# Retention values centred at their eviction, and gate tiles one ahead in both gated stages

## The chip, the cores and the metric

The kernel runs on one core of one Trainium2 chip. The metric is the device time of one execution in microseconds (us). The names used are those of the profile: PE is TensorE (matmuls; PEld its weight loads), DVE is VectorE, ACT is ScalarE, POOL is GpSimd, SP is the engine whose queue issues the weight transfers. "Line" or L with a number is a line of the kernel's source.

## What is computed

Two blocks follow one another on 512 tokens of width 1024. The first is an RWKV mixer with dilated attention, a cross attention and a feed-forward part; the change doesn't touch it. The second has two layers, and each of them does this:

```python
n = rmsnorm(x) * (1 + sc1) + sh1
u, q, k, v, g, gate_f, gate_r = split(n @ w_in)
yf = fourier_mix(u)                       # FFT over tokens and over groups of 128 features
yr = retention_branch(q, k, v, g)         # 4 heads of width 256
merged = sigmoid(gate_f) * (yf @ w_fourier) + sigmoid(gate_r) * (yr @ w_ret)
x = x + g1 * (merged @ w_out)
x = x + g2 * conv_ffn(rmsnorm(x) * (1 + sc2) + sh2)
```

In the retention branch a head's output is Y = P V, where P (512 by 512) holds the rotated queries times the rotated keys, weighed by a decay that depends on the distance in tokens. Y is then normalised over the head's 256 features (mean taken away, divided by the root of the variance plus a small number), and multiplied by silu(g). Since P acts on tokens and the mean is over features, the mean of Y over features is P times the mean of V over features.

## The kernel before

**Tiles and units.** Every projection is cut into tiles of 128 outputs by 512 tokens. Inputs and weights are held as two fp32r parts (high and low), so a tile is 8 blocks of 3 matmuls (L609 to L611), 24 in all. A value tile of the retention has tokens on the partitions and is 256 wide: 24 matmuls at L602 to L604. The weights come as units of 512 KB (128 by 1024): one unit for a 128 by 512 tile, two units for the four value tiles of a head. `RING = 4` units are in flight. For a unit u, SP's queue issues the transfer, ACT makes the high part (`cast_to`, the copy at L1207), POOL makes the low part (`low_weights`, four pieces at L558) and signals `w_low`. PE waits on `w_low` of a unit before the first matmul that reads any part of it. The list of tiles in `Plan` is the order of PE and at once the order of the units.

**When ACT casts.** ACT works in program order. `follow(t)` casts all units up to two beyond the last one of tile t. For value tiles it is less: for the first three of the four, which share their units with the next tile, nothing ahead is cast. Only `follow` of the fourth one, which stands in the program behind the eviction of the third, casts the units of the next two tiles. `gates` (L1461 on) takes the gate tiles through a sigmoid into `gate_buf` (two buffers). For each it calls `follow(t)` before and `follow(t + 1)` behind the eviction.

**Banks.** Projections rotate over PSUM banks 0 to 3; 4 to 7 serve the work between them. A tile waits until the tile four before it has been evacuated from the bank.

**Fourier stage** (L1074 to L1116). After the eight `fourier_in` tiles, whose matmuls alternate with those of the transform (`fourier_group`, over features, L1083; `fourier_tokens`, over tokens, L1098 to L1103), the gated stage `fourier_out` follows: gate tile 0 stands ahead of the last group, then come the last tokens, and `pair_stage` goes on with other 0, gate 1, other 1 and so on. "Other" is a tile of the projection that reads the Fourier result, "gate" one that reads the normed input. On ACT the cast of the third unit of `fourier_out` stands behind the `high` of the last Fourier result.

**Retention stage** (L1122 to L1171). For each head: gate tiles g, scores (L1136), query tiles of the next head, Y (L1147, banks 6 and 7), one key tile of the next head, the mean of Y by a matmul with ones (L1155, into bank 6), the other key tile, the sum of squares (L1162, bank 7), the value tiles of the next head, and the inverse deviation spread over the partitions (`spread`, L656, bank 6). For the last head there are no tiles of a next one to put between. There ACT copies Y into RY, DVE takes the mean away (L2263) and ACT squares (L1628). The inverse deviation comes from DVE (L1715), then POOL (L571, a power), then PE (L656). DVE then multiplies RY by it and by the gate (L2274, L2276), ACT and DVE split the product into high and low (L1226, L1694) for the stage `ret_out`, which pairs gate and other tiles like `fourier_out`.

**The end of `ret_out`.** The result `MERGED` is split into the same buffer A1 from which the gate tiles read, so this waits for the last gate tile (`but=1` in `split`: the last tile but one of the stage). The stage `out` reads it.

Of the kernel before, what the change touches and what calls it, by code (L numbers as in the profile page):

```python
# [15 lines left out]
P = 128  # L16
F32 = mybir.dt.float32
F32R = mybir.dt.float32r
ALU = mybir.AluOpType
# [53 lines left out]
class Plan:  # L73
# [3 lines left out]
    def __init__(self):  # L77
        self.tiles, self.stages, self.source, self.conv, self.splits = [], {}, [], [], {}
# [18 lines left out]
    def pairs(self, name, one, other, n):  # L97

        start = len(self.tiles)
        for j in range(n):  # L100
            for weight, layer, col, src in (one, other):
                u = self.unit("blocks", weight, layer, 0, col + P * j, KT, 0, KT)
                self.tiles.append(dict(blocks=[(u, P * i, i) for i in range(KT)], src=src, rows=False))
        self.stages[name] = (start, len(self.tiles))

# [35 lines left out]
def make_plan():  # L141
# [33 lines left out]
    for l in range(LAYERS):  # L175
# [3 lines left out]
        p.pairs(f"fourier_out{l}", ("w_in_2", l, 5120, "A1"), ("w_fourier_2", l, 0, "A2"), 8)  # L179
# [6 lines left out]
        p.pairs(f"ret_out{l}", ("w_in_2", l, 6144, "A1"), ("w_ret_2", l, 0, "A2"), 8)  # L186
        p.split(f"m{l}", "A1", 8, f"ret_out{l}", 1)
# [14 lines left out]
def build_program(nc, plan, ap, out):  # L202
# [19 lines left out]
    with ctx:  # L222
# [138 lines left out]
        RY = take(2, S)  # L361

# [213 lines left out]
        def _(pe):  # L576
# [103 lines left out]
            def pair_stage(name, one, other, done=0):  # L680
                t0, t1 = stages[name]
                for t in range(t0 + done, t1):
                    tile(t, splits[(one, other)[(t - t0) % 2]][0])
# [388 lines left out]
            for l in range(LAYERS):  # L1072
# [54 lines left out]
                for hd in range(XH):  # L1127
# [15 lines left out]
                    if n:  # L1143
                        pe.wait_ge(sem("ret_scaled"), n)
                    for d in range(2):
# [3 lines left out]
                        mm.then_inc(sem("ret_y"), 1)  # L1149
                    if hd + 1 < XH:  # L1150
                        tile(stages[f"ret_k{l}_{hd + 1}"][0], splits[f"n1_{l}"][0])

                    pe.wait_ge(sem("ret_copied"), 2 * n + 2)
                    for d in range(2):
                        mm = nc.tensor.matmul(banks[6][:], ones, RY[:, d, :], start=(d == 0), stop=(d == 1))  # L1155
                    mm.then_inc(sem("ret_mean"), 1)
                    if hd + 1 < XH:
                        tile(stages[f"ret_k{l}_{hd + 1}"][0] + 1, splits[f"n1_{l}"][0])
                    pe.wait_ge(sem("ret_sq"), 2 * n + 2)
                    for d in range(2):  # L1160
                        for c in range(TC):
                            mm = nc.tensor.matmul(banks[7][:, c:c + 1], ROT[:, 2 + d, c * P:(c + 1) * P], ones[:, 0:1],  # L1162
# [18 lines left out]
        def _(act):  # L1181
# [387 lines left out]
            for l in range(LAYERS):  # L1569
# [18 lines left out]
                gates(range(stages[f"fourier_out{l}"][0], stages[f"fourier_out{l}"][1], 2))  # L1588

                def take_values(hd):  # L1590
# [3 lines left out]
                    for t in range(t0, t0 + TC):  # L1594
                        follow(t)
                        take_tile(t, RV[:, t - t0, :], 256)

                for hd in range(XH):
# [30 lines left out]
                    if hd + 1 < XH:  # L1629
                        take_values(hd + 1)  # L1630
                    else:
                        follow(stages[f"ret_out{l}"][0])
                    for d in range(2):
                        high(splits[f"ret{l}"][0] + 2 * hd + d)
                gates(range(stages[f"ret_out{l}"][0], stages[f"ret_out{l}"][1], 2))
# [34 lines left out]
        def _(dve):  # L1670
# [384 lines left out]
            def gated_pairs(name, first, j0=0, j1=KT):  # L2055
                t0 = stages[name][0]
                for j in range(j0, j1):
                    g = gate()
                    evacuated(dve, t0 + 2 * j)
                    dst = MERGED[:, j, :] if first else g  # L2060
                    take_tile(t0 + 2 * j + 1, lambda b: V_.tensor_tensor(dst, g, b[:], ALU.mult))  # L2061
# [120 lines left out]
            for l in range(LAYERS):  # L2182
# [69 lines left out]
                for hd in range(XH):  # L2252
# [13 lines left out]
                    statistic(banks[7][:, 0:TC], 256, TC, EPS)  # L2266
                    if hd + 1 < XH:
                        rotate(hd + 1, "k", RKY)
                    spread_out()
                    for t in range(*stages[f"ret_g{l}_{hd}"]):  # L2270
                        evacuated(dve, t)
                    for d in range(2):
                        q = splits[f"ret{l}"][0] + 2 * hd + d
                        do(V_.tensor_tensor(RY[:, d, :], RY[:, d, :], banks[6][:], ALU.mult),  # L2274
                           "ret_scaled" if d else "vector_step")
                        do(V_.tensor_tensor(tmp[:, q % 2, :], RY[:, d, :], RG[:, d, :], ALU.mult), "tmp_ready")  # L2276
                    for d in range(2):
                        low(splits[f"ret{l}"][0] + 2 * hd + d)
                gated_pairs(f"ret_out{l}", False, 0, KT - 1)
                for j in range(KT - 1):  # L2280
# [164 lines left out]
```

## Time and profile before

| what | value |
| --- | --- |
| median of 3 runs | 3526.65 us |
| lowest and highest run | 3525.13 and 3527.23 us |
| the profiled execution | 3525.52 us |
| its span, first to last instruction | 3523.7 us |
| instructions | 44351 |
| busy share PE, PEld | 96%, 79% |
| busy share DVE, ACT, POOL | 44%, 31%, 44% |
| mean granted TensorE clock | 0.985 of full |

A busy PE in this profile is modelled and overlaps the next matmul: a 128x512 matmul is shown as 0.39 us long while the next starts 0.227 us after it. What counts for PE is therefore the distance between starts. The two layers of the second block lie from about 1625 us to 2570 us and from there to the end; their retention heads repeat with a period of 63.25 us.

### The profile page before, as it was taken

What the parts mean: (1) busy time and instruction counts of PE and PEld (TensorE: products, weight loads), DVE (VectorE), ACT (ScalarE), POOL (GpSimd) and SP (SyncE); (2) the same over time, 40 slices, a digit from 0 to 9 for tenths busy, and PEclk for the clock granted to TensorE, in tenths of its full rate; (3) what the DMA queues carried; (4) which work ended last, traced back from release to release, by engine and by line L of the source; (5) the groups of instructions that cost most, each with busy time, mean ns of one, the idle gap of its engine ahead of it and who ended that gap; (6) DMA issues with size and microseconds to landing.
All of it is one profiled execution on the core that took longest, in us unless ns stands there. A gap on an engine that the chain in (4) does not pass through costs nothing.

```text
span 3523.7 us, 44351 instructions
## 1 busy us (share of the span) xinstructions
PE 3393.0 (96%) x17184; PEld 2800.0 (79%) x17184; DVE 1536.1 (44%) x2213; ACT 1092.5 (31%) x1647; POOL 1558.0 (44%) x1926
## 2 busy tenths in 40 slices
PE   7999999999999999999999999999999999999998
PEld 7767888888887778887887877888888786878886
DVE  2246767675232366655212313633541132145434
ACT  3333333332334322223322223422332222233322
POOL 4222111211456466763443445665634442547655
PEclk9999999999999999999999999999999999999999
DMA  4111000011323266652231222223212221223222
GB/s 146 50 42 37 25 24 24 30 41 35 135 96 108 84 215 241 243 204 75 76 110 66 71 78 90 84 96 102 92 63 96 90 71 65 90 75 111 86 99 85
DMA packets 89680, 321.56 MB, mean 91 GB/s; under 512 B 9856, under 2 KB 11904, under 8 KB 89088
## 3 DMA queue, kind: packets, MB, share of 16 engines
q1 hardware_dynamic: 81936, 299.93, 25.3%
q10 hardware_dynamic: 7536, 18.80, 1.5%
q8 instruction: 137, 2.24, 0.3%
q14 instruction: 71, 0.58, 0.1%
HBM read 314.76 MB, written 3.93 MB: 90 GB/s over the span
## 4 chain that ended last, share of the span: by engine, by line
PE 62%; issue 20%; POOL 12%; DVE 4%; ACT 1%; DMA 0%; POOLq 0%; DVEq 0%; ACTq 0%; SPq 0%
PE bank L609 15%; PE bank L611 15%; PE bank L610 15%; POOL w_lo L558 12%; PE bank L769 5%; PE bank L775 2%; PE bank L1136 1%; PE bank L711 1%; PE bank L656 1%; PE bank L740 1%; PE bank L602 1%; PE bank L603 1%; PE bank L604 1%; POOL stats L571 0%; PE bank L1038 0%
## 5 line engine op out<-in xcount | busy, mean ns | idle before, releaser
L558 POOL TENSOR_TENSOR w_lo<-w_raw,w_hi 128x256 fp32r<-128x256 f32 x1888 | 1514.7, 837 | 1319.4 <-ACT w_hi L1207 1319.1
L609 PE MATMUL bank<-act,w_hi 128*128 128x512 f32 (+1 forms) x3480 | 1393.2, 400 | 48.6 <-DVE act L1694 15.6
L611 PE MATMUL bank<-act,w_lo 128*128 128x512 f32 (+1 forms) x3480 | 1357.6, 390 | 0.0
L610 PE MATMUL bank<-act,w_hi 128*128 128x512 f32 (+1 forms) x3480 | 1357.5, 390 | 0.0
L609 PEld LDWEIGHTS bank<-act,w_hi 128*128 128x128 f32 x3480 | 659.9, 190 | 204.5 <-issue 48.2
L611 PEld LDWEIGHTS bank<-act,w_lo 128*128 128x128 f32 x3480 | 659.0, 189 | 137.3
L610 PEld LDWEIGHTS bank<-act,w_hi 128*128 128x128 f32 x3480 | 660.4, 190 | 132.2 <-issue 6.2
L1207 ACT CAST w_hi<-w_raw 128x1024 fp32r<-128x1024 f32 x472 | 486.5, 1046 | 292.8 <-PE bank L611 176.1
L571 POOL TENSOR_TENSOR stats<-stats,exponent 128x8 f32<-128x8 f32 (+2 forms) x33 | 43.7, 1323 | 633.6 <-DVE stats L1715 450.1
L1215 ACT ACTIVATE arena<-bank 128x512 f32<-128x512 f32 (+2 forms) x235 | 130.3, 558 | 607.9 <-PE bank L611 470.7
L769 PE MATMUL bank<-arena 128*128 128x128 f32 (+1 forms) x1920 | 247.1, 276 | 3.5 <-DVE arena L1951 2.5
L769 PEld LDWEIGHTS bank<-arena 128*128 128x128 f32 x1920 | 231.3, 192 | 16.3 <-issue 6.6
L1694 DVE TENSOR_TENSOR act<-tmp,act 128x512 fp32r<-128x512 f32 (+1 forms) x164 | 143.8, 877 | 45.1 <-ACT act L1226 39.7
L1226 ACT CAST act<-tmp 128x512 fp32r<-128x512 f32 (+1 forms) x164 | 99.3, 606 | 200.0 <-DVE tmp L1735 46.4
L1741 DVE SCALAR_TENSOR_TENSOR arena<-bank,small,arena 128x512 f32<-128x512 f32 x64 | 48.1, 752 | 211.6 <-PE bank L611 211.6
L2061 DVE TENSOR_TENSOR arena<-arena,bank 128x512 f32<-128x512 f32 x32 | 22.0, 688 | 261.5 <-PE bank L611 259.0
L1386 ACT ACTIVATE arena<-bank 128x512 f32<-128x512 f32 x144 | 85.1, 597 | 155.2 <-PE bank L775 155.0
L2299 DVE TENSOR_SCALAR arena<-arena,params 128x512 f32<-128x512 f32 x88 | 51.4, 585 | 185.2 <-ACT arena L1215 184.8
L2134 DVE SCALAR_TENSOR_TENSOR arena<-arena,small 128x1024 f32<-128x1024 f32 x84 | 118.6, 1411 | 3.0
L602 PE MATMUL bank<-w_hi,act 128*128 128x256 f32 (+2 forms) x352 | 108.8, 309 | 4.7 <-ACT arena L1215 3.2
L775 PE MATMUL bank<-table,arena 128*128 128x128 f32 x640 | 97.0, 276 | 13.2 <-DVE arena L1951 9.0
L603 PE MATMUL bank<-w_lo,act 128*128 128x256 f32 (+2 forms) x352 | 107.1, 304 | 0.0
(239 smaller groups left out, 3009.5 us busy)
## 6 DMA issues: line engine op xcount, KB each, us to landing
w_raw<-in_weights SPq DMA_DIRECT2D x472, 512.0 KB, 3.5
arena<-in_ada SPq DMA_DIRECT2D x96, 512.0 KB, 4.3
arena<-in_strips ACTq DMA_DIRECT2D x8, 448.0 KB, 3.4
arena<-in_x ACTq DMA_DIRECT2D x4, 512.0 KB, 11.7
arena<-in_x ACTq DMA_DIRECT2D x1, 2048.0 KB, 7.9
out_y<-arena SPq DMA_DIRECT2D x1, 2048.0 KB, 6.3
y_scratch<-tmp ACTq DMA_DIRECT2D x7, 256.0 KB, 3.4
arena<-y_scratch ACTq DMA_DIRECT2D x1, 1792.0 KB, 9.1
```

The lines of the kernel that those rows point to most:

```text
L558: ins = nc.gpsimd.tensor_tensor(w_lo[:, k, cols], w_raw[:, k, cols], w_hi[:, k, cols].bitcast(F32), ALU.subtract)
L602: nc.tensor.matmul(o, xs[0], wh, start=first, stop=False)
L603: nc.tensor.matmul(o, xs[0], wl, start=False, stop=False)
L609: nc.tensor.matmul(o, wh, xh, start=first, stop=False)
L610: nc.tensor.matmul(o, wh, xl, start=False, stop=False)
L611: mm = nc.tensor.matmul(o, wl, xh, start=False, stop=last)
L769: mm = nc.tensor.matmul(b[:, w * i:w * (i + 1)], lhs[:, c, :], rhs(c), start=True, stop=True)
L775: mm = nc.tensor.transpose(b[:, P * i:P * (i + 1)], src[:, 4 * h + i, :], ident)
L1207: nc.scalar.copy(w_hi[:, k, :], w_raw[:, k, :]).then_inc(sem("w_high"), 1)
L1215: nc.scalar.activation(dst, banks[bank_of(t)][:, 0:n], func, scale=scale).then_inc(sem(f"bank_free{bank_of(t)}"), 1)
L1694: do(V_.tensor_tensor(o, x, h, ALU.subtract), "low_done")
L2134: do(V_.scalar_tensor_tensor(o, w, c_act[:, k:k + 1], o, ALU.mult, ALU.add), "ada_used")
```

## The change

A head's values are centred when they are evicted from PSUM. ACT reads a value tile once with the scale -1/256 and sums it over the features into `ret_shift`, waits for that, and reads the same bank again with the sum as bias (`take_values`). Y then has mean zero, and three steps disappear: the matmul with ones at L1155, DVE's subtraction at L2263, and ACT's square of RY. ACT instead squares directly from banks 6 and 7 and then copies them. The sum of squares goes to bank 5. `spread` moves from behind the next head's value tiles to behind its second key tile. For the last head the first two gate tiles of `ret_out` take the places of the key tiles. DVE multiplies by the gate before it waits for the spread.

The second part is the new `gated` in the plan and `gated_stage` in place of `pairs` and `pair_stage` for `fourier_out` and `ret_out`: gate 0, gate 1, other 0, gate 2, other 1, ..., gate 7, other 5, other 6, other 7. Since the plan's order is that of the units, the third unit of these stages is now that of other 0 and not that of gate 1. The split of `MERGED` waits for the last tile but two (`but=2`), and DVE runs it in three parts.

```diff
+    def gated(self, name, gate, other, n):
+
+        start, order = len(self.tiles), [(0, 0), (0, 1)]
+        for j in range(n):
+            order += [(1, j)] + ([(0, j + 2)] if j + 2 < n else [])
...
-        p.split(f"m{l}", "A1", 8, f"ret_out{l}", 1)
+        p.gated(f"ret_out{l}", ("w_in_2", l, 6144, "A1"), ("w_ret_2", l, 0, "A2"), 8)
+        p.split(f"m{l}", "A1", 8, f"ret_out{l}", 2)
...
-                tile(stages[f"fourier_out{l}"][0], splits[f"n1_{l}"][0])
+                gate_tile(f"fourier_out{l}", f"n1_{l}", 0)
                 fourier_group(KT - 1)
                 fourier_tokens(KT - 2)
+                gate_tile(f"fourier_out{l}", f"n1_{l}", 1)
                 fourier_tokens(KT - 1)
-                pair_stage(f"fourier_out{l}", f"n1_{l}", f"fourier{l}", 1)
+                gated_stage(f"fourier_out{l}", f"n1_{l}", f"fourier{l}", 2)
...
                     if hd + 1 < XH:
                         tile(stages[f"ret_k{l}_{hd + 1}"][0], splits[f"n1_{l}"][0])
-
-                    pe.wait_ge(sem("ret_copied"), 2 * n + 2)
-                    for d in range(2):
-                        mm = nc.tensor.matmul(banks[6][:], ones, RY[:, d, :], start=(d == 0), stop=(d == 1))
-                    mm.then_inc(sem("ret_mean"), 1)
-                    if hd + 1 < XH:
-                        tile(stages[f"ret_k{l}_{hd + 1}"][0] + 1, splits[f"n1_{l}"][0])
+                    else:
+                        gate_tile(f"ret_out{l}", f"n1_{l}", 0)
                     pe.wait_ge(sem("ret_sq"), 2 * n + 2)
...
+                        tile(stages[f"ret_k{l}_{hd + 1}"][0] + 1, splits[f"n1_{l}"][0])
+                    else:
+                        gate_tile(f"ret_out{l}", f"n1_{l}", 1)
+                    pe.wait_ge(sem("ret_copied"), 2 * n + 2)
+                    spread(banks[6])
+                    if hd + 1 < XH:
                         head_tiles(hd + 1, "v")
-                    else:
-                        tile(stages[f"ret_out{l}"][0], splits[f"n1_{l}"][0])
-                    spread(banks[6])
-                pair_stage(f"ret_out{l}", f"n1_{l}", f"ret{l}", 1)
+                gated_stage(f"ret_out{l}", f"n1_{l}", f"ret{l}", 2)
...
                     for t in range(t0, t0 + TC):
+                        c = t - t0
+                        src = banks[bank_of(t)][:, 0:256]
                         follow(t)
-                        take_tile(t, RV[:, t - t0, :], 256)
+                        tile_done(act, t)
+
+                        done(nc.scalar.activation(RV[:, c, :], src, ACT.Copy, scale=-1.0 / 256,
+                                                  accum_out=ret_shift[:, c:c + 1]), "ret_meant", wait=True)
+                        nc.scalar.activation(RV[:, c, :], src, ACT.Identity, bias=ret_shift[:, c:c + 1]).then_inc(
+                            sem(f"bank_free{bank_of(t)}"), 1)
...
                         act.wait_ge(sem("ret_y"), 2 * n + d + 1)
+                        done(nc.scalar.activation(ROT[:, 2 + d, :], banks[6 + d][:], ACT.Square), "ret_sq")
+                    for d in range(2):
                         done(nc.scalar.copy(RY[:, d, :], banks[6 + d][:]), "ret_copied")
...
-                    for d in range(2):
-                        act.wait_ge(sem("ret_centred"), 2 * n + d + 1)
-                        done(nc.scalar.activation(ROT[:, 2 + d, :], RY[:, d, :], ACT.Square), "ret_sq")
...
-                    dve.wait_ge(sem("ret_mean"), n + 1)
-                    for d in range(2):
-                        do(V_.scalar_tensor_tensor(RY[:, d, :], banks[6][:], -1.0 / 256, RY[:, d, :], ALU.mult,
-                                                   ALU.add), "ret_centred")
```

**Order on PE at the end of the Fourier stage.** The names are those of the matmuls over tokens (L1098 to L1103 before, L1115 to L1120 after) and of a tile's first matmul (L609, L624), whose waits name the stage: `low_done` is the Fourier result, which only other 0 reads. Before:

```order
L1098 MATMUL bank<-arena 128x128 [waits tmp_ready,f_half]
L1099 MATMUL bank<-arena 128x128
L1098 MATMUL bank<-arena 128x128
L1099 MATMUL bank<-arena 128x128
L1102 MATMUL bank<-arena 128x256
L1103 MATMUL bank<-arena 128x256
L1102 MATMUL bank<-arena 128x256
L1103 MATMUL bank<-arena 128x256
L609 MATMUL bank<-act,w_hi 128x512 [waits low_done,w_low,bank_free3]
...
L609 MATMUL bank<-act,w_hi 128x512 [waits w_low,bank_free0]
```

After:

```order
L624 MATMUL bank<-act,w_hi 128x512 [waits w_low,bank_free3]
...
L1115 MATMUL bank<-arena 128x128 [waits tmp_ready,f_half]
L1116 MATMUL bank<-arena 128x128
L1115 MATMUL bank<-arena 128x128
L1116 MATMUL bank<-arena 128x128
L1119 MATMUL bank<-arena 128x256
L1120 MATMUL bank<-arena 128x256
L1119 MATMUL bank<-arena 128x256
L1120 MATMUL bank<-arena 128x256
L624 MATMUL bank<-act,w_hi 128x512 [waits low_done,w_low,bank_free0]
```

Gate 1 has moved from behind other 0 to ahead of the last tokens; other 0 directly follows them in both.

**Order on ACT around the value tiles of the second head.** Banks are numbered; the 128x256 rows are the evictions, the two casts are the weights of the next two tiles (the g tiles). Before:

```order
L1215 ACTIVATE arena<-bank0 128x256 [waits tile_done,ret_y]
L1215 ACTIVATE arena<-bank1 128x256 [waits tile_done]
L1215 ACTIVATE arena<-bank2 128x256 [waits tile_done]
L1207 CAST w_hi<-w_raw 128x1024 [waits tile_done,w_landed3]
L1207 CAST w_hi<-w_raw 128x1024 [waits tile_done,w_landed0]
L1215 ACTIVATE arena<-bank3 128x256 [waits tile_done]
L1226 CAST act2<-tmp 128x512 [waits tile_done,tmp_ready] x2
```

After:

```order
L1617 ACTIVATE arena<-bank1 128x256 [waits tile_done]
L1619 ACTIVATE arena<-bank1,arena 128x256 [waits ret_meant]
L1617 ACTIVATE arena<-bank2 128x256 [waits tile_done]
L1619 ACTIVATE arena<-bank2,arena 128x256 [waits ret_meant]
L1224 CAST w_hi<-w_raw 128x1024 [waits tile_done,w_landed3]
L1224 CAST w_hi<-w_raw 128x1024 [waits tile_done,w_landed0]
L1617 ACTIVATE arena<-bank3 128x256 [waits tile_done]
L1619 ACTIVATE arena<-bank3,arena 128x256 [waits ret_meant]
L1243 CAST act2<-tmp 128x512 [waits tile_done,tmp_ready] x2
```

The casts keep their place behind the third tile's eviction, which now is two instructions with a wait between.

**Order on PE in the first head**, from Y (L1147, L1165) to the second head's g tiles; of each tile the row of its first matmul stands. Before:

```order
L1155 MATMUL bank6<-arena,table 128x512 [waits ret_copied]
L1155 MATMUL bank6<-arena,table 128x512
L609 MATMUL bank3<-act1,w_hi 128x512 [waits w_low,bank_free3]
...
L1162 MATMUL bank7<-table,arena 128x1 [waits ret_sq]
L1162 MATMUL bank7<-table,arena 128x1 x7
L602 MATMUL bank0<-w_hi,act1 128x256 [waits w_low,bank_free0]
...
L656 MATMUL bank6<-table,stats 128x128 [waits inverse_ready]
L656 MATMUL bank6<-table,stats 128x128 x3
L609 MATMUL bank0<-act1,w_hi 128x512 [waits w_low,bank_free0]
```

After:

```order
L1176 MATMUL bank5<-table,arena 128x1 [waits ret_sq]
L1176 MATMUL bank5<-table,arena 128x1 x7
L624 MATMUL bank3<-act1,w_hi 128x512 [waits w_low,bank_free3]
...
L671 MATMUL bank6<-table,stats 128x128 [waits inverse_ready,ret_copied]
L671 MATMUL bank6<-table,stats 128x128 x3
L617 MATMUL bank0<-w_hi,act1 128x256 [waits w_low,bank_free0]
...
L624 MATMUL bank0<-act1,w_hi 128x512 [waits w_low,bank_free0]
```

The mean (L1155) is gone, and the spread (L656, now L671) stands ahead of the value tiles, so that the g tile directly follows them.

## Rows read from the trace of the kernel before

**Rows 1.** The page's busy times: us, share of the span, instructions.

```profile
PE 3393.0 (96%) x17184; PEld 2800.0 (79%) x17184; DVE 1536.1 (44%) x2213; ACT 1092.5 (31%) x1647; POOL 1558.0 (44%) x1926
```

**Rows 2.** Waits of PE: us in total, times, longest us.

```profile
PE bank L609 <- POOL w_lo L558: 15.0, 14, 3.0
```

**Rows 3.** Timeline of PE, the mean's matmuls in the first head: start, length, instruction.

```profile
1869.38 1.88 PE L1155 MATMUL bank<-arena,table 128*128 128x512 f32 x4
1870.69 0.79 PE L609 MATMUL bank<-act,w_hi 128*128 128x512 f32 x1
1871.33 0.39 PE L610 MATMUL bank<-act,w_hi 128*128 128x512 f32 x1
```

**Rows 4.** Timeline of PE, the last head of the first layer, from Y on.

```profile
2037.13 7.11 PE L1147 MATMUL bank<-arena 128*128 128x512 f32 x16 [1.05 <-DVE arena L2257]
2044.92 1.98 PE L1155 MATMUL bank<-arena,table 128*128 128x512 f32 x4 [0.68 <-ACT arena L1622]
2049.14 1.95 PE L1162 MATMUL bank<-table,arena 128*128 128x1 f32 x16 [2.24 <-ACT arena L1628]
2050.95 0.47 PE L609 MATMUL bank<-act,w_hi 128*128 128x512 f32 x1
```

**Rows 5.** Timeline of PE, from value tiles to g tiles, first and second head.

```profile
1826.53 0.28 PE L604 MATMUL bank<-w_hi,act 128*128 128x256 f32 x1
1828.32 0.47 PE L609 MATMUL bank<-act,w_hi 128*128 128x512 f32 x1 [1.51 <-POOL w_lo L558]
...
1889.88 1.05 PE L656 MATMUL bank<-table,stats 128*128 128x128 f32 x8
1891.56 0.47 PE L609 MATMUL bank<-act,w_hi 128*128 128x512 f32 x1 [0.62 <-POOL w_lo L558]
```

**Rows 6.** Timelines of ACT and POOL there: third value tile, casts, low parts.

```profile
1887.20 0.38 ACT L1215 ACTIVATE arena<-bank 128x256 f32<-128x256 f32 x1 [2.50 <-PE bank L604]
1887.49 1.99 ACT L1207 CAST w_hi<-w_raw 128x1024 fp32r<-128x1024 f32 x2
...
1888.60 4.65 POOL L558 TENSOR_TENSOR w_lo<-w_raw,w_hi 128x256 fp32r<-128x256 f32 x6 [8.83 <-ACT w_hi L1207]
```

**Rows 7.** Timeline of ACT, an eviction with a sum, in the cross attention.

```profile
1117.02 0.47 ACT L1517 ACTIVATE arena<-bank,arena 128x256 f32<-128x256 f32 x1
1117.38 0.20 ACT L1517 ACTIVATION_READ_ACCUMULATOR arena<-bank,arena 128x1 f32 x1
```

**Rows 8.** Timelines of PE, ACT and POOL, end of the first Fourier stage.

```profile
1711.08 0.58 PE L609 MATMUL bank<-act,w_hi 128*128 128x512 f32 x1
1717.09 0.47 PE L609 MATMUL bank<-act,w_hi 128*128 128x512 f32 x1 [0.21 <-POOL w_lo L558]
...
1712.98 1.05 ACT L1207 CAST w_hi<-w_raw 128x1024 fp32r<-128x1024 f32 x1
...
1714.11 4.29 POOL L558 TENSOR_TENSOR w_lo<-w_raw,w_hi 128x256 fp32r<-128x256 f32 x6 [13.57 <-ACT w_hi L1207]
```

**Rows 9.** Timeline of PE: first matmuls behind two waits of nearly equal length.

```profile
198.05 0.67 PE L609 MATMUL bank<-act,w_hi 128*128 128x512 f32 x1 [1.87 <-ACT arena L1215]
236.28 0.50 PE L609 MATMUL bank<-act,w_hi 128*128 128x512 f32 x1 [1.88 <-ACT arena L1215]
```

**Rows 10.** Windows: stretch, us, five engines' busy us (instructions), PE clock, DMA share.

```profile
1261.00:1266.60 5.60, 5.60 (x14) 4.36 (x14) 5.46 (x5) 1.05 (x1) 5.60 (x5) 0.50 0.77 273
2052.20:2055.20 3.00, 3.00 (x9) 2.37 (x8) 0.00 (x0) 0.00 (x0) 3.00 (x5) 0.52 0.00 0
2996.00:3000.40 4.40, 4.40 (x12) 3.38 (x11) 0.00 (x0) 0.00 (x0) 3.73 (x5) 0.50 0.00 0
```

**Rows 11.** Timelines of PE and ACT at the start of the first layer's stage out.

```profile
2147.09 0.50 PE L609 MATMUL bank<-act,w_hi 128*128 128x512 f32 x1 [1.43 <-DVE act L1694]
...
2145.62 0.62 ACT L1226 CAST act<-arena 128x512 fp32r<-128x512 f32 x1 [4.94 <-DVE small L2067]
2146.15 1.04 ACT L1207 CAST w_hi<-w_raw 128x1024 fp32r<-128x1024 f32 x1
```

More of the change, by code:

```diff
@@ L77, in __init__ @@
     def __init__(self):
-        self.tiles, self.stages, self.source, self.conv, self.splits = [], {}, [], [], {}
+        self.tiles, self.stages, self.source, self.conv, self.splits, self.gates = [], {}, [], [], {}, {}
     def unit(self, *source):
@@ L104, in pairs @@
         self.stages[name] = (start, len(self.tiles))
+    def gated(self, name, gate, other, n):
+        start, order = len(self.tiles), [(0, 0), (0, 1)]
+        for j in range(n):
+            order += [(1, j)] + ([(0, j + 2)] if j + 2 < n else [])
+        at = {}
+        for which, j in order:
+            weight, layer, col, src = (gate, other)[which]
+            u = self.unit("blocks", weight, layer, 0, col + P * j, KT, 0, KT)
+            at[which, j] = len(self.tiles)
+            self.tiles.append(dict(blocks=[(u, P * i, i) for i in range(KT)], src=src, rows=False))
+        self.stages[name] = (start, len(self.tiles))
+        self.gates[name] = [at[0, j] for j in range(n)], [at[1, j] for j in range(n)]
     def token_major(self, name, weight, layer, col, cols, token_tiles, src="A1"):
@@ L178, in make_plan @@
         p.split(f"fourier{l}", "A2", 8, before)
-        p.pairs(f"fourier_out{l}", ("w_in_2", l, 5120, "A1"), ("w_fourier_2", l, 0, "A2"), 8)
+        p.gated(f"fourier_out{l}", ("w_in_2", l, 5120, "A1"), ("w_fourier_2", l, 0, "A2"), 8)
         for h in range(XH):
@@ L361, in build_program @@
         RY = take(2, S)
+        ret_shift = take(TC)
         free_at[0] = base
@@ L678, in stage, with gate_tile, gated_stage @@
                     spread(banks[4])
[L680 to L683, printed above, removed]
+            def gate_tile(name, split, j):
+                tile(plan.gates[name][0][j], splits[split][0])
+            def gated_stage(name, one, other, done=0):
+                for t in range(stages[name][0] + done, stages[name][1]):
+                    tile(t, splits[one if t in plan.gates[name][0] else other][0])
             pe.wait_ge(sem("ld_table"), 16)
@@ L1142, in _ @@
                     pe.wait_ge(sem("ret_masked"), TC * (n + 1))
-                    if n:
-                        pe.wait_ge(sem("ret_scaled"), n)
+                    if hd:
+                        pe.wait_ge(sem("tmp_ready"), splits[f"ret{l}"][0] + 2 * hd)
                     for d in range(2):
@@ L1161, in _ @@
                         for c in range(TC):
-                            mm = nc.tensor.matmul(banks[7][:, c:c + 1], ROT[:, 2 + d, c * P:(c + 1) * P], ones[:, 0:1],
+                            mm = nc.tensor.matmul(banks[5][:, c:c + 1], ROT[:, 2 + d, c * P:(c + 1) * P], ones[:, 0:1],
                                                   start=(d == 0 and c == 0), stop=(d == 1), skip_group_check=True)
@@ L1587, in _ @@
                         high(splits[f"fourier{l}"][0] + j - 2)
-                gates(range(stages[f"fourier_out{l}"][0], stages[f"fourier_out{l}"][1], 2))
+                gates(plan.gates[f"fourier_out{l}"][0])
                 def take_values(hd):
@@ L1625, in _ @@
                             follow(t)
-                    for d in range(2):
-                        act.wait_ge(sem("ret_centred"), 2 * n + d + 1)
-                        done(nc.scalar.activation(ROT[:, 2 + d, :], RY[:, d, :], ACT.Square), "ret_sq")
-                    if hd + 1 < XH:
                         take_values(hd + 1)
                     else:
-                        follow(stages[f"ret_out{l}"][0])
+                        for t in plan.gates[f"ret_out{l}"][0][0:2]:
+                            follow(t)
                     for d in range(2):
                         high(splits[f"ret{l}"][0] + 2 * hd + d)
-                gates(range(stages[f"ret_out{l}"][0], stages[f"ret_out{l}"][1], 2))
+                gates(plan.gates[f"ret_out{l}"][0])
                 for j in range(KT):
```

26 lines of the change are left out of this document (12 added, 14 removed).

## The prediction

> **What bounds the kernel now.** I read the page first: PE is busy 96% of the span, the others under half [rows 1]. That share flatters PE, since it counts overlapping lengths, so I then read starts in the timeline. In a projection tile the matmuls start 0.227 us apart (24 of them: 5.44 us), and nearly the whole span is such a stream. So any matmul taken from PE's order is gained, and any time in which PE has to wait is lost. The view of waits says what PE waits for: in 14 places the low part of a weight unit, which POOL makes, is the last to come, 15.0 us in all [rows 2]. The change takes matmuls out and fills the empty places of the last heads, but it also lengthens an eviction and reorders units, and both stand ahead of casts on ACT. So I went through four places: the mean's matmuls, the last head, the passage from value tiles to g tiles, and the start of the Fourier stage's gated tiles.
>
> **1. The mean's matmuls go.** They start at 1869.38; the second matmul of the next tile starts at 1871.33, where one step of 0.227 would be due [rows 3]. 1871.33 - 1869.38 - 0.227 = 1.72 us per head. They lie on PE with nothing beside them. 8 heads: **-13.8 us**. DVE's and ACT's steps that go with them are beside PE and cost nothing, except in the last head.
>
> **2. The last heads.** Y starts at 2037.13 and takes 16 steps of 0.43 us (the pace of the mean's four), so it is through at 2044.00. The mean starts at 2044.92: 0.9 us lost. It is through 1.72 later, at 2046.64, and the sum of squares starts at 2049.14: 2.5 lost [rows 4]. Then the granted clock falls to half for some 3.3 us, about 1.6 us of loss (8 steps of 0.427 in place of 0.227; the window of 3.0 us shows nine matmuls at 0.52) [rows 10]. Together 5.0 us. The second layer shows the same two waits, but there the half level already covers the sum of squares (0.9 us more) and then 4.4 us of tile (12 matmuls at 0.50 [rows 10], 12 times 0.2 = 2.4): 6.7 us. After the change a gate tile of 5.44 us stands in each of the two places. ACT needs two squares of 0.6 us for the first and DVE and POOL about 1.5 us for the second, so both are covered. The gate tiles are only moved. **-11.7 us**. What stays is the wait of 1.05 us before Y [rows 4], for the scores have nothing between them and Y.
>
> **3. From value tiles to g tiles.** In the first head nothing stands between. The last value matmul starts at 1826.53, one step is 0.12, and the g tile starts at 1828.32: 1.67 us lost, while POOL makes the low part [rows 5]. The chain behind it is in the second head: the third value tile's eviction starts at 1887.20, the cast 0.29 later, POOL at 1888.60 and PE at 1891.56 [rows 5, 6]. Everything in it hangs on the eviction, and this becomes longer. A read with a sum is 0.47 long and its accumulator read ends 0.56 behind its start [rows 7]. ACT then waits for its own signal (not in this trace; between nothing and the 0.11 that POOL takes behind its cast [rows 6]; I take 0.1), reads again for 0.47 (a biased read; 0.38 without) and starts the cast 0.1 before that ends (the overlap of 1887.49 with 1887.20 + 0.38 [rows 6]): 0.56 + 0.1 + 0.47 - 0.1 = 1.03, less 0.29 is 0.7 (bounds 0.55 and 0.9). Queued behind this wait on ACT are just these two casts, and PE waits for them. So 0.7 us more in each of 8 heads.
>
> In the three heads per layer that have a next one the spread now stands elsewhere. Before, it took its time (0.81 us from its start to the next one's, the same as in the last head) inside the 1.67 us that PE would have waited anyway: 1889.88 to 1891.56 is 1.68 [rows 5]. Moved behind the second key tile it costs 0.81 us of its own, and the wait comes back whole. The inverse deviation itself is in time there: 5.44 us of key tile against about 1.5 on DVE and POOL, whose low parts for the values are done some 9 us after Y. So: 8 times 0.7 plus 6 times 0.8, **+10.4 us**. That undoes most of step 1.
>
> **4. The clock behind these waits.** PE's printed idle there grows from 1.51 to about 2.2 us. The trace has no such row in dense tiles. After 1.87 us of idle the first matmul is 0.67 long and the next ones run at half level; after 1.88 it is 0.50 and nothing falls [rows 9]; after 1.51 nothing falls [rows 5]; after 2.24 (with waits shortly before) and after 3.0 us (at 1260.66, the longest of the waits for POOL) it falls [rows 2, 4, 10]. So at 2.2 us it is open, and I take half of the 8 places. A fall costs 0.2 us per matmul: 1.6, 2.4 and 2.9 (14 matmuls) in the three stretches [rows 10], mean 2.3. **+9.2 us** (bounds 0 and 23).
>
> The Trainium skill (TensorE: Matmul & The Clock Gate, "Why this matters for your kernels") asks for no idle gap above about 3 us to keep the full clock. By it this step is 0. The trace speaks against it with the row of 1.87 us.
>
> **5. The Fourier stage's gated tiles.** Other 0 starts at 1711.08, directly behind the last tokens; gate 1, which is the third unit, starts at 1717.09, and POOL's low part is what it waits for [rows 8]. The chain: last tokens, DVE's copies, ACT's `high`, only then the cast of the third unit at 1712.98, POOL from 1714.11 on, PE 6.0 us behind the last tokens. Before, this is hidden by other 0 (5.6 us), all but 0.37 us. After, the third unit is that of other 0, which stands directly behind the last tokens, and ACT's order is as it was: the cast stands behind the `high` of the last result. Gate 1, which used to follow, now lies ahead of the last tokens and hides nothing of this chain. So PE waits 6.0 us in place of 0.37: 5.6 us per layer, 11.3. Behind 3.0 us of waiting it fell [rows 2, 10], so behind 6 I take a fall from full speed (2.4 GHz) to half (1.2 GHz) as certain: 2.3 us each. **+15.9 us**.
>
> **6. The end of `ret_out`.** The stage `out` waits 1.6 us within its first tile for the last part of `MERGED` (1.43 printed) [rows 11]. One more tile between the last gate and `out` takes that away. But ACT now casts the second unit of `out` only behind the last `high`: that ends about 2.4 us into the first tile, plus cast 1.0 and POOL 2.9 makes 6.3 against 5.44, so 0.9 us lost. Before, this unit was cast behind the last gate and only the third one at 2146.15 [rows 11]. **-1.4 us** for both layers.
>
> **The sum** is -13.8 - 11.7 + 10.4 + 9.2 + 15.9 - 1.4 = +8.6 us. Against the profiled execution's 3525.5 that is 3534.1. The median is 1.1 higher: **3535 us**.
>
> **Rivals.**
> A, the clock holds in all eight places of step 4. For it: 1.88 us without a fall. Against: 1.87 with one, and 2.2 is longer. It gives 3535 - 9 = 3526, no change. This is also what the skill's rule gives.
> B, faster: other 0's unit is in time in the Fourier stage. Step 5 falls away and the sum is -7.3: 3519. It decides at the cast's place: it would have to be made before the last tokens end, that is ahead of the last `high`. The order on ACT and the 6.0 us of rows 8 speak against it; for it only that ring and transfer would allow it.
> C, dearer: the clock falls at all or nearly all eight places, or for two long stretches at each, or the read with a sum is at its upper bound: 8 times 2.3 is 9 more, 0.2 times 8 is 1.6 more: 3546.
>
> **How the numbers follow.** Forecast 0.50 (3530 to 3540), A 0.29, B 0.06, C 0.15. Without A and C the unknowns are the eviction (1.6 us to either side), the clock in step 5 (1 to 3 us each) and other waits that the new phases move, so 5 us to either side. The range holds A's middle less 2 and C's middle: 3524 to 3546. A measurement of this kernel tells about 0.2% (7 us) from no change, so the bound to slower is 3533.7: the lower third of the forecast (0.15) and A are the same; slower is 0.35 + 0.15; faster is most of B, 0.05, and the rest counts as the same.
>
> **What would show it.** Right: PE has no L1155 and 1.7 us less from Y to the second key tile. The last heads have no wait behind Y. The g tiles wait 2.2 us on POOL's low part in all 8 heads. The first other tile of `fourier_out` waits 6 us on it, with half clock behind. Wrong: if that wait is short, step 5 falls and with it the sign of the sum; if the eviction pair takes over 1.3 us or under 0.8, step 3; if the granted clock stays at full behind all g waits, A.

## The result, and the profile after

| what | before | after |
| --- | --- | --- |
| median | 3525.93 us (21 runs) | 3533.72 us (21 runs) |
| lowest and highest | 3519.60 and 3528.76 us | 3528.92 and 3538.69 us |
| profiled execution | 3525.52 us | 3528.92 us |

The ratio is 1.0022, with a 95% interval of 1.0015 to 1.0029: the change makes the kernel 7.8 us slower. 3535 us with 8.6 us of loss were forecast. Note that the profiled execution of after is the lowest of its 21 runs, so its rows add up to a smaller loss, 3.4 us, than the medians do. That gap is taken up below.

The page of after, busy times. PE has 32 matmuls fewer than before and is 12.4 us less busy, though the kernel is slower [rows 1].

```profile
PE 3380.6 (96%) x17152; PEld 2793.3 (79%) x17152; DVE 1524.5 (43%) x2197; ACT 1108.9 (31%) x1711; POOL 1553.4 (44%) x1926
```

The view of PE's waits of after: us in total, times, longest.

```profile
PE bank L624 <- POOL w_lo L573: 26.0, 15, 3.0
...
PE bank L624 <- issue: 11.1, 2, 5.5
```

The first line was 15.0 us in 14 places [rows 2]. The second is new. Its name, "issue", tells nothing; the timelines of PE, ACT and POOL at the end of the first Fourier stage of after show what it is (start, length, instruction, idle before it and its releaser):

```profile
1717.47 0.59 PE L1120 MATMUL bank<-arena 128*128 128x256 f32 x2
1723.61 0.77 PE L624 MATMUL bank<-act,w_hi 128*128 128x512 f32 x1 [5.54 <-issue]
...
1719.09 0.62 ACT L1243 CAST act<-tmp 128x512 fp32r<-128x512 f32 x1 [7.46 <-DVE tmp L2248]
1719.62 1.04 ACT L1224 CAST w_hi<-w_raw 128x1024 fp32r<-128x1024 f32 x1
...
1720.73 3.57 POOL L573 TENSOR_TENSOR w_lo<-w_raw,w_hi 128x256 fp32r<-128x256 f32 x5 [19.02 <-ACT w_hi L1224]
```

The last matmul of the last tokens starts at about 1717.7 and other 0 starts at 1723.61, 5.9 us later, behind the same chain as in [rows 8]: the result's `high`, the cast at 1719.62, POOL's low part from 1720.73 on. The first matmul behind the wait is 0.77 us long, so it runs at the lower of TensorE's two levels (0.47 us behind a wait at full level).

The same engines from the second head's value tiles to its g tiles, in after:

```profile
1895.28 0.38 ACT L1617 ACTIVATE arena<-bank 128x256 f32<-128x256 f32 x1 [1.90 <-PE bank L619]
1895.56 0.19 ACT L1617 ACTIVATION_READ_ACCUMULATOR arena<-bank 128x1 f32 x1
1895.78 0.47 ACT L1619 ACTIVATE arena<-bank,arena 128x256 f32<-128x256 f32 x1
1896.15 1.98 ACT L1224 CAST w_hi<-w_raw 128x1024 fp32r<-128x1024 f32 x2
...
1897.27 2.11 POOL L573 TENSOR_TENSOR w_lo<-w_raw,w_hi 128x256 fp32r<-128x256 f32 x3 [15.10 <-ACT w_hi L1224]
...
1897.84 0.28 PE L619 MATMUL bank<-w_hi,act 128*128 128x256 f32 x1
1900.21 0.47 PE L624 MATMUL bank<-act,w_hi 128*128 128x512 f32 x1 [2.10 <-POOL w_lo L573]
```

From the third eviction's start to the cast it is 0.87 us, where it was 0.29 [rows 6]; PE waits 2.10 us (printed), where it waited 0.62 behind the spread and 1.51 without one [rows 5]. All eight heads print 2.09 or 2.10.

In the timeline of PE in the last head of the first layer, neither the sum of squares (L1176) nor the spread behind the second gate tile has a wait left. The first gate tile starts at 2055.05, the second at 2062.61:

```profile
2048.51 7.10 PE L1165 MATMUL bank<-arena 128*128 128x512 f32 x16 [1.05 <-DVE arena L2279]
2055.05 0.80 PE L624 MATMUL bank<-act,w_hi 128*128 128x512 f32 x1
...
2060.90 1.84 PE L1176 MATMUL bank<-table,arena 128*128 128x1 f32 x16
2062.61 0.48 PE L624 MATMUL bank<-act,w_hi 128*128 128x512 f32 x1
```

And at the start of the stage `out` the wait is 0.89 us, from 1.43 [rows 11], now on the low part of the second unit:

```profile
2151.73 0.47 PE L624 MATMUL bank<-act,w_hi 128*128 128x512 f32 x1 [0.89 <-POOL w_lo L573]
```

The windows of after behind other 0's wait and behind two of the g waits, and one stretch without a wait for comparison (columns as in [rows 10]; the clock is the third number from the end):

```profile
1724.00:1727.40 3.40, 3.40 (x9) 2.63 (x9) 0.00 (x0) 0.93 (x1) 3.40 (x6) 0.50 0.50 157
1838.00:1841.00 3.00, 3.00 (x15) 2.49 (x14) 0.00 (x0) 0.40 (x1) 3.00 (x5) 1.00 0.61 186
1902.00:1905.00 3.00, 3.00 (x8) 2.31 (x8) 0.00 (x0) 0.00 (x0) 3.00 (x5) 0.50 0.56 167
2028.40:2031.40 3.00, 3.00 (x9) 2.32 (x8) 0.99 (x1) 0.34 (x1) 3.00 (x5) 0.50 0.81 265
```

The clock was at half behind 4 of the 8 g waits of this execution (near 1902, 2028, 2909 and 2974 us), 1.7 us of loss each, and at full behind the other four, though the waits are of the same length to 0.01 us.

### The profile page after: what moved, and what is told of

The parts are those of the page before. It is cut to its first block, busy times and chain, and to the rows that moved or that the text cites. A ratio compares the mean times of both kernels' runs of the same rounds, so it can differ in the third digit from the quotient of the medians.

```text
span 3527.1 us, 44345 instructions
## 1 busy us (share of the span) xinstructions
PE 3380.6 (96%) x17152; PEld 2793.3 (79%) x17152; DVE 1524.5 (43%) x2197; ACT 1108.9 (31%) x1711; POOL 1553.4 (44%) x1926
## 4 chain that ended last, share of the span: by engine, by line
PE 67%; issue 17%; POOL 11%; DVE 5%; ACT 1%; DMA 0%; POOLq 0%; DVEq 0%; ACTq 0%; SPq 0%
PE bank L624 16%; PE bank L626 16%; PE bank L625 16%; POOL w_lo L573 10%; PE bank L786 5%; PE bank L792 2%; PE bank L1154 1%; PE bank L1100 1%; PE bank L728 1%; PE bank L671 1%; PE bank L757 1%; POOL stats L586 0%; PE bank L1055 0%; PE bank L939 0%; PE bank L958 0%
## 5 line engine op out<-in xcount | busy, mean ns | idle before, releaser
L624 PE MATMUL bank<-act,w_hi 128*128 128x512 f32 (+1 forms) x3480 | 1392.7, 400 | 69.4 <-POOL w_lo L573 26.0
L624 PEld LDWEIGHTS bank<-act,w_hi 128*128 128x128 f32 x3480 | 660.2, 190 | 226.9 <-issue 71.3
L1232 ACT ACTIVATE arena<-bank 128x512 f32<-128x512 f32 (+2 forms) x203 | 118.0, 586 | 516.6 <-PE bank L626 495.8
```

What stands on the lines that cost most here:

```text
L624: nc.tensor.matmul(o, wh, xh, start=first, stop=False)
L1232: nc.scalar.activation(dst, banks[bank_of(t)][:, 0:n], func, scale=scale).then_inc(sem(f"bank_free{bank_of(t)}"), 1)
```

## The experiments

Each run starts from the changed kernel, but for the last. The kernel before, timed beside them, had medians of 3525.2, 3525.7 and 3525.4 us in the three groups of runs. A ratio is to that. A distance to after goes from one group of runs to another, and before itself differs by up to 0.7 us between the groups (3525.9 beside after), so such a distance is good to about 1 us.

**e1. The Fourier stage alone back in its old order.** It tests step 5 by taking it out, and leaves the rest of the change.

```diff
...
-        p.gated(f"fourier_out{l}", ...
+        p.pairs(f"fourier_out{l}", ...
...
-                gate_tile(f"fourier_out{l}", f"n1_{l}", 1)
                 fourier_tokens(KT - 1)
-                gated_stage(f"fourier_out{l}", f"n1_{l}", f"fourier{l}", 2)
+                gated_stage(f"fourier_out{l}", f"n1_{l}", f"fourier{l}", 1)
```

> The changed kernel with the Fourier stage's gated tiles back in the order before (other 0 is again the second unit, gate 1 stands behind it); all else as changed. Theory of step 5: the wait of 5.9 us behind the last tokens and the half clock behind it go, in both layers, and 0.4 us comes back: 5.5 + 2 = 7.5 per layer, so 15 us under the changed kernel: about 3518.7, 7 us faster than before. Rival (the order of gates costs nothing, the loss is elsewhere): 3533.7.

Measured: 3515.8 us, ratio 0.9975 (0.9964 to 0.9986), 17.9 us under after. In its view of waits the line on "issue" for the tiles is gone and the g waits stay:

```profile
PE bank L625 <- POOL w_lo L574: 26.8, 16, 3.0
```

So the Fourier half of the change costs all of the loss and more; the retention half gains 9.4 us. Against before timed beside each, the Fourier half is 17.2 us (7.8 + 9.4), 1 to 2 us above the forecast of 15.9.

**e4. The order stays, other 0's unit is cast ahead of the last `high`.** If the chain on ACT is the cause, its place alone must do.

```diff
                         take_tile(t0 + j, UF[:, j % 2, :])
+                        if j == KT - 1:
+                            cast_to(tiles[plan.gates[f"fourier_out{l}"][1][0]]["blocks"][0][0])
```

> The changed kernel, its order kept, with one cast moved on ACT: the third unit of the Fourier stage's gated tiles is cast behind the eviction of the last fourier_in tile, ahead of the last two high parts. Theory: what makes PE wait is the cast's place and not the tiles' order, so this gives the same as putting the order back: about 3518.5, and PE's row behind the last tokens has no wait. Rival (the unit can't be in time because its ring slot, its transfer or POOL is late): a wait of some us stays, 3525 or more.

Measured: 3523.0 us, ratio 0.9993 (0.9983 to 1.0002), so the same as before; 10.7 us under after, 4.5 less than expected. The timeline of PE in e4 shows the miss, one tile on:

```profile
1723.33 0.47 PE L624 MATMUL bank<-act,w_hi 128*128 128x512 f32 x1 [2.05 <-POOL w_lo L573]
```

Other 0 no longer waits, but gate 2 does, for the fourth unit. Its cast stands behind ACT's load of the sigmoid's table and the eviction of gate 0, and had been hidden by the wait of 5.9 us. The cause of step 5 stands; what was missing in my expectation is the next in line.

**e3. The centring alone**, both gated stages in the old order (the cut shows `ret_out`; the Fourier stage is put back as in e1). The last head then has one gate tile, as before.

```diff
...
-        p.gated(f"ret_out{l}", ...
-        p.split(f"m{l}", "A1", 8, f"ret_out{l}", 2)
+        p.pairs(f"ret_out{l}", ...
+        p.split(f"m{l}", "A1", 8, f"ret_out{l}", 1)
...
-                    else:
-                        gate_tile(f"ret_out{l}", f"n1_{l}", 1)
                     pe.wait_ge(sem("ret_copied"), 2 * n + 2)
```

> Before plus the centring at the eviction and the spread's new place alone; both gated stages in the order before, one gate tile in the last head. Theory: as with the Fourier order put back (3518.7), but in the last head the spread directly follows the sum of squares and waits about 1.6 us per layer, and the stage out has its 1.6 us wait in place of 0.9: +3.2 + 1.4, about 3523, 3 us faster than before. Rival (the eviction's waits and the clock cost more than the mean and the last head give): 3526 or more.

Measured: 3528.0 us, ratio 1.0013 (1.0004 to 1.0023), 5 us above what was expected. The timeline of PE in the last head of e3:

```profile
2060.40 1.45 PE L672 MATMUL bank<-table,stats 128*128 128x128 f32 x7 [2.00 <-POOL stats L587]
```

The inverse deviation takes 2 us with nothing beside it, and the clock fell behind it in both layers, 1.7 us each, and behind 6 of the 8 g waits. So centring by itself gains nothing; the new order of `ret_out` is what makes the retention half a gain (12.1 us between e3 and e1). The two profiled executions, 12.2 us apart, say where: 4.3 us in each layer lie between the last head and the end of `out` (this wait, the clock behind it, and 0.5 at the start of `out`), 1.7 is one more fall at a g tile, and 1.7 had arisen ahead of the second block, where the kernels are the same.

**e8. One plain copy in place of the eviction pair.** It leaves out the centring, so it is timed for the eviction alone: step 3 without the longer eviction, the spread where the change put it.

```diff
-                        done(nc.scalar.activation(RV[:, c, :], src, ACT.Copy, scale=-1.0 / 256,
-                                                  accum_out=ret_shift[:, c:c + 1]), "ret_meant", wait=True)
-                        nc.scalar.activation(RV[:, c, :], src, ACT.Identity, bias=ret_shift[:, c:c + 1]).then_inc(
-                            sem(f"bank_free{bank_of(t)}"), 1)
+                        nc.scalar.activation(RV[:, c, :], src, ACT.Copy).then_inc(sem(f"bank_free{bank_of(t)}"), 1)
```

> The changed kernel with the value tiles evicted by one plain copy: the centring is left out (Y keeps its mean). Theory of steps 3 and 4: the chain to the g tiles' low part is 0.58 us shorter (0.87 from the eviction's start to the cast's, 0.29 before), 8 times: 4.6 us; and the printed waits are 1.5 us again, where no fall of the clock was seen: about four falls of 1.7 us go. 3533.7 - 4.6 - 6.8 = 3522. Rival (the falls have nothing to do with the wait's length): 3529.

Measured: 3520.4 us, ratio 0.9987 (0.9978 to 0.9996), some 13 us under after. PE at the second head's g tile in e8:

```profile
1899.58 0.47 PE L624 MATMUL bank<-act,w_hi 128*128 128x512 f32 x1 [1.50 <-POOL w_lo L573]
```

The wait is 0.6 us shorter (8 times that is 4.8), and the clock fell behind none of the eight. What is left of the 13 us is 8.5. Falls of 1.7 us would make that five, where the profiled execution of after had four.

**e5. The casts for the g tiles ahead of the third eviction.** This takes the whole wait away, with the pair as it is.

```diff
                         follow(t)
+                        if c == 2:
+                            cast_to(min(max(u for u, _, _ in tiles[t]["blocks"]) + 2, n_units - 1))
                         tile_done(act, t)
```

> The changed kernel with the casts of the two g tiles' weights moved on ACT from behind to ahead of the third value tile's eviction. Theory: PE's wait from value tiles to g tiles (2.27 us between starts, 2.10 printed) hangs on ACT's order alone; it goes in all 8 heads, 18 us, and with it the falls of the clock, 7 us: about 3509. Rival 1: POOL or the ring is late all the same and some wait stays. Rival 2: the two casts (2 us) now delay the third eviction and with it a bank: PE waits elsewhere, under 10 us gained, 3524.

Measured: 3507.6 us, ratio 0.9948 (0.9933 to 0.9963), 26 us under after. The waits of PE in e5:

```profile
PE bank L624 <- issue: 11.1, 2, 5.5
...
PE bank L624 <- POOL w_lo L573: 9.3, 7, 3.0
```

None at a g tile is left, and no half clock there. Per head the passage had cost 26 / 8 = 3.3 us: 2.1 to 2.2 of waiting, and the rest, 1.1, for the clock. So ACT's order, and not the work on ACT, is the price of the pair.

**e10. The spread back behind the value tiles.** The other part of step 3.

```diff
                     pe.wait_ge(sem("ret_copied"), 2 * n + 2)
-                    spread(banks[6])
                     if hd + 1 < XH:
                         head_tiles(hd + 1, "v")
+                    spread(banks[6])
```

> The changed kernel with the spread of the inverse deviation back behind the next head's value tiles. Theory of step 3: there it lies inside the wait for the g tiles' low part and costs nothing: 6 times 0.81 = 4.9 us less; the printed wait in these six heads falls from 2.1 to about 1.2 us and the falls of the clock in them go, about 5 us: 3524. Rival (the spread costs the same in either place): 3533.

Measured: 3520.6 us, ratio 0.9986 (0.9977 to 0.9996), 13 us under after. The second head's g tile in e10:

```profile
1900.87 0.47 PE L624 MATMUL bank<-act,w_hi 128*128 128x512 f32 x1 [1.20 <-POOL w_lo L573]
```

The wait went from 2.10 to 1.20 in six heads, since the spread again fills a part of it, and the clock fell behind none of these six, but behind both first heads, where nothing stands between and the wait stays 2.09. It is 3.4 us more than was expected: six spreads are 4.9, and the 8.3 left would be five falls, as in e8.

**e6. e4 and e5 together.** It asks whether the two terms add.

```diff
+                        if j == KT - 1:
+                            cast_to(tiles[plan.gates[f"fourier_out{l}"][1][0]]["blocks"][0][0])
...
+                        if c == 2:
+                            cast_to(min(max(u for u, _, _ in tiles[t]["blocks"]) + 2, n_units - 1))
```

> The changed kernel with both moves of casts: the g tiles' ahead of the third eviction, and the third unit of the Fourier stage's gated tiles behind the last fourier_in tile. Theory: they add up, -25 - 15: about 3494, 32 us under before. Rival: they share a cause and give less than the sum, 3505.

Measured: 3495.4 us, ratio 0.9911 (0.9895 to 0.9928). They do: 38.4 us under after, where e4 and e5 have 10.7 and 26.1. Gate 2's wait stays, here without a fall of the clock:

```profile
1726.87 0.47 PE L624 MATMUL bank<-act,w_hi 128*128 128x512 f32 x1 [2.06 <-POOL w_lo L573]
```

**e11. e5, and both the third and the fourth unit cast ahead of the last `high`.** It tests the reading of e4's miss.

```diff
+                        if j == KT - 1:
+                            cast_to(tiles[plan.gates[f"fourier_out{l}"][0][2]]["blocks"][0][0])
```

> Both moves of casts, and the fourth unit of the Fourier stage's gated tiles (gate 2) is cast with the third, ahead of the last high parts. In the run with both moves gate 2 waited 2.06 us (printed; 2.2 between starts) in each layer, because its cast stood behind gate 0's table load and eviction. Theory: this wait goes: 4.4 us under that run (3495.4), about 3491. Rival: POOL makes the third and fourth unit one after the other and is late with the fourth all the same: 3495.

Measured: 3490.7 us, ratio 0.9903 (0.9889 to 0.9917): 4.7 us under e6, and the wait at gate 2 is gone. Against e5 the Fourier term is 17.0 us.

**e12. e11, and the second unit of `out` cast behind the last gate, ahead of the splits of `MERGED`.**

```diff
                 gates(plan.gates[f"ret_out{l}"][0])
+                cast_to(tiles[stages[f"out{l}"][0] + 1]["blocks"][0][0])
```

> The kernel with the three units cast early, and the second unit of the stage out is cast right behind the last gate tile, ahead of the eight high parts of the merged result. Theory of step 6: the wait of 0.89 us (printed) at that unit goes in both layers, 2 us less: about 3489. Rival: the cast delays the high parts by 1 us and the first tile of out waits for them instead: 3491.

Measured: 3488.6 us, ratio 0.9897 (0.9882 to 0.9913), 2.1 us under e11. This is the kernel that beats both, 37 us under before. Its waits of PE for low parts, and the second head's passage, where the g tile follows one step (0.12 us) behind the last value matmul:

```profile
PE bank L624 <- POOL w_lo L573: 8.4, 5, 3.0
```

```profile
1887.39 0.28 PE L619 MATMUL bank<-w_hi,act 128*128 128x256 f32 x1
1887.51 0.40 PE L624 MATMUL bank<-act,w_hi 128*128 128x512 f32 x1
```

**e13. The kernel before, with e5's early casts.** How much of this has nothing to do with the change?

```diff
                         follow(t)
+                        if t - t0 == 2:
+                            cast_to(min(max(u for u, _, _ in tiles[t]["blocks"]) + 2, n_units - 1))
                         take_tile(t, RV[:, t - t0, :], 256)
```

> The kernel before with one edit: the g tiles' casts ahead of the third value tile's eviction. Theory: its waits there were 1.67 us between starts in two heads and 0.87 behind the spread in six: 8.6 us, about 3517. Rival: the waits before were hidden by something else and it stays at 3525. Beside the changed kernel with the same edit (3507.6) it tells what the centring gives once the passage from value tiles to g tiles costs neither kernel anything.

Measured: 3515.1 us, ratio 0.9968 (0.9958 to 0.9979). So 10 of the 37 us were to be had in the kernel before. With this edit in both, the changed kernel is the faster one, 3507.6 (e5) against 3515.1. The wait at the g tiles alone decides the sign of the change, and so does the wait at other 0 alone (e1).

## Why the prediction was right

The forecast was 8.6 us of loss, the medians show 7.8, and it came by the mechanisms named. Not all sizes were right, and two errors offset each other, so a part of the closeness is luck. The forecast was also added to the profiled execution of before, and the profiled execution of after shows only 3.4 of the 8.6.

**Step 1 holds.** L1155 is gone, and from the last matmul of Y the key tile goes on at once. No run took it out alone, but the tile starts show it: from the first head's g tile to the second's first value matmul it was 49.97 us (1828.32 to 1878.29) and is 49.12 (1837.24 to 1886.36), 0.85 less although the spread's 0.81 is now inside. That is 1.7 us per head, as forecast.

**Step 2 holds.** No wait stands behind Y in either last head, in the rows above and in the second layer. e3 shows what the second gate tile hides: with one tile the spread waits 2.00 us. The wait before Y is 1.05, as forecast. From Y to the start of `out` the profiled execution of after gains 6.9 us in the first layer and 8.4 in the second; less 1.7 each for step 1 that is 11.8, where 11.7 was forecast.

**Step 3 was a little too dear.** The eviction pair delays the cast by 0.58 us, where 0.7 was taken: the cast starts 0.87 behind the eviction, where the working had 1.03. Two terms were too large. The read with its accumulator's read ends 0.47 behind its start and not 0.56, since the read itself is 0.38 long here and not 0.47 as in the cross attention. And ACT's wait for its own signal, 1895.75 to 1895.78, costs 0.03 and not 0.1 us. 8 times 0.12 is 1 us. The spread's 0.81 is as said. In the timeline of PE in after:

```profile
1885.55 1.05 PE L671 MATMUL bank<-table,stats 128*128 128x128 f32 x8
1886.36 0.36 PE L617 MATMUL bank<-w_hi,act 128*128 128x256 f32 x1
```

It costs the 0.81 us, and the wait is whole again; e10 takes both back.

**Step 4 was right in sum, by two errors.** I took a fall in half of the places at 2.3 us each, 1.15 per place. Counted over the profiles of after, e1, e3, e4 and e10, the clock fell behind 22 of 34 g waits of 2.1 us (4 of 8, 5 of 8, 6 of 8, 5 of 8, 2 of 2), and one fall costs 1.7 us: 22 / 34 times 1.7 is 1.1 per place. So it falls more often and costs less. In the profiled execution of after alone it fell in half of the places, as taken, and the step is 6.8 us there and not 9.2. By the medians e5, e8 and e10 leave 8.1 to 8.7 us for the clock. e8 (1.50 us, none of 8) and e10 (1.20, none of 6) show that it hangs on the length of the wait, as the step argued from the rows of 1.51 and 1.87. Rival A, the clock that holds, is out. The rule of the Trainium skill ("TensorE: Matmul & The Clock Gate", "Why this matters for your kernels"), no idle gap above about 3 us, would have given 3526; here waits of 2.1 us cost the clock in two of three places, so the measurement decides against it.

The gap between the medians and the profiled execution of after, 4.8 us, stays open. More falls at the g tiles could make it (three by 1.7 us; five in all by e5, e8 and e10), but only one execution has a profile. Its two fastest executions have the highest mean granted clock, 0.985, and the slowest has the lowest, 0.981; between them the two don't go together. The clock also moves in places that the change doesn't touch. In the cross attention before had it at half from 1261 to 1266.6 us [rows 10], and the profiled execution of after had it at full in the same stretch:

```profile
1261.00:1266.60 5.60, 5.05 (x22) 4.24 (x23) 5.46 (x5) 1.53 (x2) 5.60 (x5) 1.00 0.87 319
```

**Step 5 holds in mechanism and nearly in size.** The wait is 5.9 us (6.0 forecast). The clock behind it is the part that was too dear: 1.7 us in the first layer and 1.9 in the second, where 2.3 were forecast. 5.9 - 0.37 + 1.8 = 7.3 us per layer. The whole Fourier stage agrees, from its first matmul over features to the first value tile: it took 171.4 us before and takes 178.6 and 178.7 in the profile of after, 14.5 for both layers, and 171.4 again in e1. The runs that take it out give 17.2 to 17.9 (e1) and 17.0 (e5 to e11, where the stage goes from 179.0 to 170.9 us, 16.3 by the rows, since e11 removes the 0.37 as well). So 0.7 us of the second is open and some 3 us of the first; the gap between after's median and its profiled execution may be in it. Rival B fails where it was said to decide: the cast stands behind the last `high`.

**Step 6 holds.** 0.89 us is printed, as forecast, the second tile of `out` comes 0.7 us nearer in each layer, 1.3 where 1.4 was forecast, and e12 gives back 2.1 where the two waits are 1.8.

**The sum, with the measured terms**: -13.8 - 11.7 + (8 x 0.58 + 6 x 0.81 = 9.5) + (8 x 1.1 = 8.8) + 17 (the runs' value) - 1.4 = +8.4 us, against 7.8 measured. Of the profiled execution alone, with 4 falls (6.8) and the rows' 14.5, it is +3.9. By the tile starts the two layers cost 2.7 and 1.3 us from the Fourier stage to the second tile of `out`, 4.0 in all. The 3.4 us between the two profiled executions hold two things more: 1.2 us had arisen when the Fourier stage began (1643.73 before, 1644.91 after), and 1.7 come back behind `out`, where the clock was at half for a shorter time in after. No step of the sum stands for either.

**What I didn't see** is the second in line. In e4 the fourth unit became late as soon as the third was in time: a wait of 2.05 us in each layer that I had not priced, 4.4 us by the starts, against a miss of 4.5. In e3 I had priced the spread's wait, at 1.6 us for 2.0, but not the clock behind it, 1.7 us in each layer: 4.2 of the 5 us.

## What to carry to other kernels

Where an engine casts weights ahead by the index of the tile that it has just evacuated, reordering tiles changes which unit is cast in time, and lengthening an eviction that stands ahead of the cast can be paid by PE in full, as here (0.58 us more on ACT, 0.59 more of waiting), although the engine is a third busy. Put the cast ahead of the eviction before judging such a change: here three added calls of `cast_to` took the kernel from 8 us slower to 37 us faster. When you remove a wait, ask what the next unit behind it waits for, and price the clock behind any idle of about 2 us.

## What the runs showed of the hardware

The clock of TensorE fell behind 22 of 34 waits of 2.1 us in dense streams of matmuls, behind 3 of 6 of 2.00 to 2.06 us (e3 2 of 2, e4 1 of 2, e6 0 of 2), and behind 14 shorter ones (1.20 and 1.50 us) never; the half level then cost 1.7 us each time. Equal waits in equal surroundings differ in this within one execution. That this is what makes a kernel's time spread is not shown: after spreads over 9.8 us in 21 runs, but before, without a g wait above 1.51 us, over 9.2 in 21, and e8, without a fall at a g tile in its profile, over 9.0 in ten. e12 spreads over 2.3, in four runs.

A read with a sum, its accumulator's read and a second read with this sum as bias take 0.38, 0.19 and 0.47 us for 128x256 on ACT, and the engine's wait for its own signal between them costs 0.03 us.
